# Delta rule on one Trainium2 core: the triangular inverse kept on one side and transposed for the other, with half the columns in each level

## The reference, cut to what matters

```python
a_mat = jnp.where(strict, jnp.einsum('bnhcd,bnhsd->bnhcs', k_beta, k) * gamma, 0.0) \
    + jnp.eye(CHUNK, dtype=jnp.float32)
rhs = jnp.concatenate([v * beta[..., None], k_beta * jnp.exp(G)[..., None]], axis=-1)
sol = lax.linalg.triangular_solve(a_mat, rhs, left_side=True, lower=True, unit_diagonal=True)
...
def step(S, inp):
    qd, w_c, u_c, at, kt, dec = inp
    v_new = u_c - jnp.einsum('bhcd,bhde->bhce', w_c, S)
    o = jnp.einsum('bhcd,bhde->bhce', qd, S) + jnp.einsum('bhcs,bhse->bhce', at, v_new)
    S = S * dec[..., None, None] + jnp.einsum('bhcd,bhce->bhde', kt, v_new)
    return S, o
```

## Time and profile before

| | us |
|---|---|
| median of 3 runs | 1982.2 |
| lowest and highest of them | 1977.0, 1984.09 |
| the profiled execution, device time | 1981.22 |
| its span in the profile | 1979.9 |
| PE busy | 1785.5 (90%) |
| DVE busy | 1232.4 (62%) |
| ACT busy | 718.6 (36%) |
| POOL busy | 434.1 (22%) |

### The profile page before, as it was taken

One profiled execution on the slowest core, in us unless ns is written; L12 is line 12 of the kernel. 1 busy time (PEld: TensorE's weight loads), 2 busy tenths in 40 slices (PEclk: granted clock), 3 DMA queues, 4 the chain that ended last, 5 costly groups with the idle time before them and its releaser, 6 DMA issues. The chain is left out here.

```text
span 1979.9 us, 23713 instructions
## 1 busy us (share of the span) xinstructions
PE 1785.5 (90%) x9424; PEld 1353.9 (68%) x9424; DVE 1232.4 (62%) x2155; ACT 718.6 (36%) x1243; POOL 434.1 (22%) x373
## 2 busy tenths in 40 slices
PE   7989999999999999998989999997878787887878
PEld 6869988977799879888979777893333333333333
DVE  4766655665576557654464445688776677667754
ACT  3545534344355346642342344343221122212211
POOL 0330000310000000004022000033555545454541
PEclk9989999999999999989989979998889988888889
DMA  6334555444445543412221211479999999999995
GB/s 261 110 114 149 191 183 180 170 153 166 165 176 190 182 177 110 149 64 80 92 68 62 86 62 67 170 287 421 422 421 421 422 422 421 422 422 421 421 422 245
DMA packets 62621, 453.76 MB, mean 229 GB/s; under 512 B 6944, under 2 KB 7072, under 8 KB 7856
## 3 DMA queue, kind: packets, MB, share of 16 engines
q0 software_dynamic: 36864, 268.45, 32.6%
q1 hardware_dynamic: 25040, 178.27, 25.4%
q10 hardware_dynamic: 608, 5.53, 0.7%
HBM read 451.18 MB, written 1.05 MB: 228 GB/s over the span
## 5 line engine op out<-in xcount | busy, mean ns | idle before, releaser
L2346 PE MATMUL banks<-uv_rows,diag 128*128 128x512 f32 x1024 | 509.8, 662 | 126.9 <-ACT diag L2395 122.5
L553 DVE TENSOR_TENSOR weights_lo<-weights,weights_hi 128x1024 fp32r<-128x1024 f32 x336 | 422.7, 1299 | 284.9 <-ACT weights_hi L544 282.3
L2346 PEld LDWEIGHTS banks<-uv_rows,diag 128*128 128x128 f32 x1024 | 215.4, 214 | 420.6 <-issue 269.3
L544 ACT ACTIVATE weights_hi<-weights 128x1024 fp32r<-128x1024 f32 x336 | 336.7, 1051 | 388.5 <-PE banks L560 380.2
L558 PE MATMUL banks<-x_hi,weights_hi 128*128 128x256 f32 (+1 forms) x1472 | 428.6, 291 | 6.7 <-DVE weights_lo L553 3.6
L560 PE MATMUL banks<-x_hi,weights_lo 128*128 128x256 f32 (+1 forms) x1472 | 422.0, 287 | 0.0
L559 PE MATMUL banks<-x_lo,weights_hi 128*128 128x256 f32 (+1 forms) x1472 | 421.8, 287 | 0.0
L2482 DVE CUSTOM_DVE_ANT_0 uv_rows<-uv_rows,tokens 128x1024 f32<-128x1024 f32 x256 | 306.4, 1224 | 165.1 <-DMA uv_rows<-expert_uv,index 165.0
L2505 POOL DMA_INDIRECT uv_rows<-expert_uv,index x256 | 310.9, 1214 | 339.9 <-PE banks L2346 285.5
L558 PEld LDWEIGHTS banks<-x_hi,weights_hi 128*128 128x128 f32 x1472 | 283.9, 193 | 16.8 <-issue 8.2
L560 PEld LDWEIGHTS banks<-x_hi,weights_lo 128*128 128x128 f32 x1472 | 283.6, 193 | 0.0
(11 more groups left out here) (379 smaller groups left out, 2239.8 us busy)
## 6 DMA issues: line engine op xcount, KB each, us to landing
weights<-weights SPq DMA_DIRECT2D x168, 1024.0 KB, 4.8
uv_rows<-expert_uv,index POOLq DMA_INDIRECT x256, 18.5
sb_first<-constants_first ACTq DMA_DIRECT2D x1, 1920.0 KB, 8.6
sb_always<-constants_always ACTq DMA_DIRECT2D x1, 1659.0 KB, 15.1
sb_peer<-constants_peer ACTq DMA_DIRECT2D x1, 1544.0 KB, 6.5
h<-x SPq DMA_DIRECT2D x1, 1024.0 KB, 5.7
out<-h SPq DMA_DIRECT2D x4, 256.0 KB, 4.7
sb_now<-constants_now ACTq DMA_DIRECT2D x1, 216.0 KB, 4.7
```

The costliest lines, as they stand in the source:

```text
L544: self.act.activation(self.w_hi[b % SLOTS][:, f], self.raw[b % SLOTS][:, f], ACT.Copy).then_inc(self.hi_made, 1)
L553: self.dve.tensor_tensor(self.w_lo[b % SLOTS][:, f], self.raw[b % SLOTS][:, f], self.w_hi[b % SLOTS][:, f], ALU.subtract).then_inc(self.lo ...
L2346: mm = pe.matmul(self.bank(2 * t + half), self.diag[:, k, :], self.uv[n % NUV][:, f], start=(u < NT and k == 0), stop=(u >= UNITS - NT and ...
```

## The change

- Only dTT is kept. dT is made anew in each level: PE transposes dTT into the tile's second bank, ACT copies it out as dT next to dM. The second product of step 4 (line 1797) and DVE's subtraction from dT (line 1965) are gone.
- In each level only the columns of the second blocks of each pair change in dTT. `second` names these columns (half of them), and M, dM, the remaining product and the subtraction are made for them alone: 64 columns instead of 128 for each head.
- In level 6 of tiles 1 and 2 (`whole`) the matrices are taken as squares of 64 by 64: A's lower left block is read where it stands, without the mask, and dB is not made.
- dTT starts as identity minus (dAT times "next"), two DVE operations for each tile inside the loop over tiles. The copies of the identity, the first dT, the first dB by the mask of level 0, POOL's part of it and the wait of all engines for T0 and T0_pool are gone. PE waits for the three dA instead, then for the tile's T0. POOL makes dB of level 1 for each tile as soon as that tile's dA is there and the last products with dgam are done.

The diff, cut to its core:

```diff
+    def second(self, x, lvl):
+        return x.rearrange("p h (b two s) -> p h b two s", two=2, s=1 << lvl)[:, :, :, 1, :]
+    def joined(self, lvl, t, j):
+        n = TILES[t][1]
+        return self.level_bank(t, j)[:, 0:HG * n // 2].rearrange("p (h b s) -> p h b s", h=HG, s=1 << lvl)
+    def whole(self, lvl, t):
+        return t > 0 and lvl == self.LEVELS[t] - 1
...
 tensor_delta:
-        wait("T0", 2)
-        wait("T0_pool", 1)
+        wait("A", 3)
         for lvl in range(1, 7):
             for t in self.active(lvl):
...
-                wait("B", i)
                 if lvl > 1:
                     wait("T", self.level_count(lvl - 1, t))
+                else:
+                    wait("T0", t + 1)
                 for hh in range(HG):
-                    mm = pe.matmul(ps[:, hh * n:(hh + 1) * n], b[:, hh, :], tt[:, hh, :], start=True, stop=True)
+                    if self.whole(lvl, t):
+                        pe.transpose(turned[0:half, hh * half:(hh + 1) * half], tt[0:half, hh, 0:half], C["ident"][0:half, 0:half])
+                    else:
+                        pe.transpose(turned[:, hh * n:(hh + 1) * n], tt[:, hh, :], C["ident"][0:n, 0:n])
+                if not self.whole(lvl, t):
+                    wait("B", i)
+                for hh in range(HG):
+                    if self.whole(lvl, t):
+                        mm = pe.matmul(ps[0:half, hh, 0, :], a[half:P, hh, 0:half], tt[half:P, hh, half:P], start=True, stop=True)
+                    else:
+                        mm = pe.matmul(ps[:, hh], b[:, hh, :], self.second(tt, lvl)[:, hh], start=True, stop=True)
...
                 for hh in range(HG):
-                    if not last:
-                        pe.matmul(pz[:, hh * n:(hh + 1) * n], m1[:, hh, :], tm[:, hh, :], start=True, stop=True)
-                    mm = pe.matmul(pzt[:, hh * n:(hh + 1) * n], tm[:, hh, :], m1[:, hh, :], start=True, stop=True)
+                    if self.whole(lvl, t):
+                        mm = pe.matmul(pzt[0:half, hh, 0, :], tm[0:half, hh, 0:half], m1[0:half, hh, 0:half], start=True, stop=True)
+                    else:
+                        mm = pe.matmul(pzt[:, hh], tm[:, hh, :], m1[:, hh, 0:n // 2].rearrange("p (b s) -> p b s", s=1 << lvl),
+                                       start=True, stop=True)
...
 scalar_delta:
-                act.activation(self.of("dM", t), self.level_bank(t, 0)[:, 0:HG * n].rearrange("p (h n) -> p h n", h=HG),
+                act.activation(self.of("dM", t)[0:rows, :, 0:n // 2],
+                               self.level_bank(t, 0)[0:rows, 0:HG * n // 2].rearrange("p (h n) -> p h n", h=HG), ACT.Copy)
+                act.activation(self.of("dT", t)[0:rows, :, 0:cols],
+                               self.level_bank(t, 1)[0:rows, 0:HG * cols].rearrange("p (h n) -> p h n", h=HG),
                                ACT.Copy).then_inc(d["M1"].sem, 1)
...
 vector_delta:
-            step.of(dve.tensor_copy(self.of("dT", t), self.each("ident", n)))
-            dve.tensor_copy(self.of("dTT", t), self.each("ident", n)).then_inc(d["eye"].sem, 1)
...
+            wait("masked", t + 1)
+            step.of(dve.tensor_tensor(self.of("dTT", t), at, self.each("next", n), ALU.mult))
             dve.wait_ge(step.sem, step.n)
-            step.of(dve.tensor_tensor(self.of("dT", t), self.of("dT", t), self.of("dB", t), ALU.subtract))
-            step.of(dve.tensor_tensor(self.of("dM", t), self.of("dAT", t), self.each("next", n), ALU.mult))
-            dve.wait_ge(step.sem, step.n)
-            dve.tensor_tensor(self.of("dTT", t), self.of("dTT", t), self.of("dM", t), ALU.subtract).then_inc(d["T0"].sem, 1)
+            dve.tensor_tensor(self.of("dTT", t), self.each("ident", n), self.of("dTT", t), ALU.subtract).then_inc(d["T0"].sem, 1)
...
-                if not final:
-                    step.of(dve.tensor_tensor(tm, tm, pz[:, 0:HG * n].rearrange("p (h n) -> p h n", h=HG), ALU.subtract))
-                    dve.wait_ge(step.sem, step.n)
-                dve.tensor_tensor(tt, tt, pzt[:, 0:HG * n].rearrange("p (h n) -> p h n", h=HG), ALU.subtract).then_inc(d["T"].sem, 1)
+                wait(*(("T", self.level_count(lvl - 1, t)) if lvl > 1 else ("T0", t + 1)))
+                dve.tensor_tensor(tt, tt, pzt, ALU.subtract).then_inc(d["T"].sem, 1)
...
 gpsimd_delta:
+        wait("prod_used", 3)
         for lvl in range(1, 7):
             for t in self.active(lvl):
+                if self.whole(lvl, t):
+                    continue
                 n = TILES[t][1]
                 if lvl > 1:
                     wait("M", self.level_count(lvl - 1, t))
+                else:
+                    wait("A", t + 1)
                 pool.tensor_tensor(self.of("dB", t), self.of("dA", t), self.each("merge", n, lvl * P), ALU.mult).then_inc(d["B"].sem, 1)
```

More of the change, by code:

```diff
@@ L492, in signals @@
         names = {"rows": 3, "rows_used": 3, "gam": 3, "prod": 3, "prod_used": 3, "turn": 3, "turn_used": 3, "masked": 3, "attn": 2,
-                 "back": 3, "A": 3, "eye": 3, "T0": 2, "T0_pool": 1, "B": 15, "M": 15, "M1": 15, "Z": 15, "T": 15, "ks": 2,
+                 "back": 3, "A": 3, "T0": 3, "B": 13, "M": 15, "M1": 15, "Z": 15, "T": 15, "ks": 2,
                  "rhs": 2, "pv": 3, "vn": 3, "sp": 2, "po": 2, "state": 2, "out": 2}
@@ L1865, in scalar_delta @@
         fill(7)
[L1866 to L1867 removed]
         for lvl in range(1, 7):
             for t in self.active(lvl):
[L1870 removed]
+                n, i, whole = TILES[t][1], self.level_count(lvl, t), self.whole(lvl, t)
+                rows, cols = (P // 2, P // 2) if whole else (n, n)
                 act.wait_ge(d["M"].sem, d["M"].at(group, i))
[L1872 removed]
+                act.activation(self.of("dM", t)[0:rows, :, 0:n // 2],
+                               self.level_bank(t, 0)[0:rows, 0:HG * n // 2].rearrange("p (h n) -> p h n", h=HG), ACT.Copy)
+                act.activation(self.of("dT", t)[0:rows, :, 0:cols],
+                               self.level_bank(t, 1)[0:rows, 0:HG * cols].rearrange("p (h n) -> p h n", h=HG),
                                ACT.Copy).then_inc(d["M1"].sem, 1)
@@ L1957, in vector_delta @@
             for t in self.active(lvl):
-                n, i, final = TILES[t][1], self.level_count(lvl, t), lvl == self.LEVELS[t] - 1
-                tm, tt = self.of("dT", t), self.of("dTT", t)
-                pz, pzt = self.level_bank(t, 1), self.level_bank(t, 2)
+                i = self.level_count(lvl, t)
+                tt, pzt = self.second(self.of("dTT", t), lvl), self.joined(lvl, t, 2)
+                if self.whole(lvl, t):
+                    tt, pzt = (x[0:P // 2] for x in (tt, pzt))
                 wait("Z", i)
-                if lvl > 1:
-                    wait("T", self.level_count(lvl - 1, t))
-                if not final:
-                    step.of(dve.tensor_tensor(tm, tm, pz[:, 0:HG * n].rearrange("p (h n) -> p h n", h=HG), ALU.subtract))
-                    dve.wait_ge(step.sem, step.n)
-                dve.tensor_tensor(tt, tt, pzt[:, 0:HG * n].rearrange("p (h n) -> p h n", h=HG), ALU.subtract).then_inc(d["T"].sem, 1)
+                wait(*(("T", self.level_count(lvl - 1, t)) if lvl > 1 else ("T0", t + 1)))
+                dve.tensor_tensor(tt, tt, pzt, ALU.subtract).then_inc(d["T"].sem, 1)
             fill(7 + 2 * lvl)
@@ L2004, in wait @@
             pool.wait_ge(d[name].sem, d[name].at(group, n))
-        n = TILES[2][1]
-        wait("A", 3)
-        wait("eye", 3)
-        wait("masked", 3)
-        step.of(pool.tensor_tensor(self.of("dB", 2), self.of("dA", 2), self.each("merge", n), ALU.mult))
-        pool.wait_ge(step.sem, step.n)
-        step.of(pool.tensor_tensor(self.of("dT", 2), self.of("dT", 2), self.of("dB", 2), ALU.subtract))
-        step.of(pool.tensor_tensor(self.of("dM", 2), self.of("dAT", 2), self.each("next", n), ALU.mult))
-        pool.wait_ge(step.sem, step.n)
-        pool.tensor_tensor(self.of("dTT", 2), self.of("dTT", 2), self.of("dM", 2), ALU.subtract).then_inc(d["T0_pool"].sem, 1)
-        wait("T0", 2)
-        wait("T0_pool", 1)
+        wait("prod_used", 3)
         for lvl in range(1, 7):
             for t in self.active(lvl):
+                if self.whole(lvl, t):
+                    continue
                 n = TILES[t][1]
```

22 lines of the change are left out of this document (5 added, 17 removed).

## The result

| | before | after |
|---|---|---|
| median of 4 runs, us | 1981.54 | 1954.84 |
| lowest and highest | 1977.0, 1984.09 | 1952.89, 1965.39 |
| the profiled execution, device time | 1981.22 | 1965.39 |
| its span | 1979.9 | 1964.1 |

After over before is 0.9875, with a 95% interval of 0.9839 to 0.9911. The kernel is faster by 26.7 us between medians, where 38.6 were forecast. 1954.84 lies inside the range, 12 us above the forecast and near the times of rivals 1 and 2. The profiled execution is the slowest of the four, so its total is compared with nothing here; its stretches are. One execution of a later kernel (3522.3 us, at half clock throughout) was in a disturbed state and is left out everywhere.

A forecast was written before the change was run, and what follows sets the result against it. PE's own program order bounds the levels, except waits for POOL before level 1. 25.0 + 2.6 + 9.5 + 4.0 - 2.5 = 38.6 us less gives 1943 us; own range 1938 to 1949, wide range 1936 to 1961.

The forecast's parts named there:

- rival 1: Handovers, POOL's masks and splits collide; each of the 12 levels loses 1 us more than forecast: 1955 us, chance 0.16.
- rival 2: Half the columns don't take half the time; stationary load or strided read sets 0.112 us a record: 1959, chance 0.15.
- Part 1: Levels 1 to 5, tiles 1 and 2: half columns, 0.124 us a product, no second product; 25.0 us less.
- Part 2: Level 6 in 64 by 64 squares: 1.15 us against 1.79, four times; 2.6 us less (1.4 to 2.7).
- Part 4: Start of level 1: PE's waits for POOL's dB go, all three inputs being early; 9.5 us less.
- Part 5: Without the 4 us pause before level 1, the half clock behind it should not come: 4.0 us less, at least 0.
- rival 4: Slower: thin work drops the clock to 1.2 GHz, 2018 us, chance 0.03; partial form, group 1 levels, 1949, 0.07.
- Part 6: Handovers to ACT and DVE in the levels make PE wait, against 3.8 us of old idle time: net cost 2.5 us.
- Part 7: Weight stream: with two slots, the chain of ACT and DVE making a block's parts fits in the levels; nothing counted.
- The last sign: The prediction is wrong if the time between the delta rule and the end changes, which the change doesn't touch.

## Why the prediction was right, and where its sum was not

The sign, the range and the mechanisms of the start held; the size did not. The forecast's own range, 1938 to 1949, missed the time. The wide range held it because it took in rivals 1 and 2; that the time lies at rival 1's 1955 is chance, since that rival's mechanism didn't appear. The gain is accounted for at equal clock, from the traces of before and after. In the levels the length less half of the half-clock time went from 62.9 to 56.6 us in group 0 (64.6 less 1.7; 60.0 less 3.4) and from 48.3 (51.1 less 2.8) to 40.5 in group 1: 14.1 us. The stretches from the first key product to level 1, read the same way, went down by 8.2 us. These are their rows before and after:

```profile
855.22:898.91 43.69, 37.47 (x269) 33.84 (x269) 26.65 (x49) 20.98 (x47) 8.49 (x6) 0.96 0.25 93
990.30:1034.09 43.79, 37.76 (x270) 34.00 (x270) 29.08 (x50) 21.90 (x47) 7.41 (x6) 0.91 0.21 73
```

```profile
852.90:892.45 39.55, 37.40 (x269) 33.81 (x269) 22.29 (x39) 18.67 (x44) 4.28 (x3) 0.96 0.27 99
980.40:1022.93 42.53, 40.41 (x270) 36.84 (x268) 26.06 (x42) 21.43 (x46) 3.65 (x3) 0.84 0.19 67
```

The stretches of group 0 differ by 4.1 us at one clock, 0.96. In group 1 the length times the clock is 39.8 and 35.7, 4.1 less. DVE's and POOL's busy time fell as their copies and masks went. Together with the levels that is 22.3 us.

**Part 1 is the step that failed: "I take 0.062, so 0.124 a product".** The record of 128 stationary and 64 moving columns steps at 0.112 us, the upper bound. The part gives 9.0 us, not 25.0; what PE saves is the second product of step 4, less the transposes, and no columns. The choice between the bounds went by the row with the same load, but that row's operation was a transpose, and the sizes of a row don't carry over to another kind of operation. This is rival 2 in its full form, and the Trainium skill, page "TensorE: Matmul & The Clock Gate", section "LDWEIGHTS (loading the stationary operand)", had it: by its rule a load of 128 columns takes 107 ns whatever the partitions, and the products here, at 0.112 on 128 partitions and on 8, agree. The transposes with the same 128 columns, at 0.063, do not. I had set that one row against the rule where the rule applied.

**Part 2.** The square level takes 0.94 us for transposes and M and about 0.52 for the product (8 records at 0.065), 1.46 a tile where I took 1.15. Against the 1.79 of before, four times, it saves 1.3 us of PE's time, not 2.6. The run without squares doesn't measure this sum, since it puts half columns at full height there and not the two full products of before: its tile takes about 2.2 us, 2.9 more in the four places, where the traces have 2.7 and the means 4.

**Part 4.** All three conditions were early, as forecast. The waits of 8.0 and 1.5 us are gone, and the stretches ahead of level 1 are 8.2 us shorter at equal clock. By the runs with one part alone the start is worth more than this part and part 5 together, 18 us against 13.5.

**Part 5.** Half right. The half clock behind the pause is gone, and in the kernel with the new start and the old levels a run has 20 us less of it, worth 7 to 10 us. In the changed kernel it came back: behind level 6 of both groups, and ahead of level 1 of group 1, where the rows above go from 0.91 to 0.84. The mean half-clock time of a run is 251 to 259 us, against 254: the net is nothing, not 4.0. This is the partial form of rival 4, at other places. In group 0 the clock fell behind the wait of 1.0 us in all three traces of the changed kernel and in none with that wait filled, but two other kernels with the same wait kept it. So what makes it fall stayed open, in group 0 in part and in group 1 wholly: there it also falls with full columns and with level 6 at full height.

**Part 6.** The handovers cost less. The table of waits of the changed kernel, PE between 860 and 1100 us, has this row for the products of level 6:

```profile
PE banks L1819 <- ACT dT L1897: 1.3, 2, 1.0
```

That, 1.3 us in two waits, and 0.5 us before the recurrence is all, 1.8 us. Level 6 of group 0 waits 1.0 us instead of about 1.8. The 0.27 and 0.45 us that I expected between M and the product in levels 2, 3 and 5 are not there. M of tile 2, which PE makes meanwhile, takes 0.84 us instead of the 0.50 that Part 1 gave it, and the product of tile 1 is longer in the same way; that this is what covers them was argued, not tried. Against 3.8 us of old idle time the part gives 2.0 us more instead of costing 2.5. Rival 1 is out: no wait for POOL's dB stands in the levels. (Its argument that DVE's load falls by two thirds was too high: in the levels it fell from 53.4 to 29.7 us.)

**The sum with these terms**, parts 1, 2, 4, 6 and 5 in this order, is 9.0 + 1.3 + 9.5 + 2.0 + 0 = 21.8 us, against 22.3 in the two traces' delta rule and 22 to 25 by the three ratios. Two errors of the forecast had opposite signs, the pace (16 too much) and the handovers (4.5 too little). That the two partly cancel is luck and not foresight: with the pace right and all else as forecast it would have been rival 2's 1959. Part 7 held: the projections' weights didn't hold PE in the levels. The last sign, the time behind the levels, is 894.7 us before and 900.6, 894.0 and 898.7 in the three traces of the changed kernel. It lies around the old value, and the spread is as large within one kernel.

## What to carry to other kernels

With 128 stationary columns, a step of f32 products was shortened only when the stationary side shrank with the moving one; take a triangular or block structure as squares, not as column halves. When a product's pace is read from a neighbouring row, check the kind of operation as well as the sizes: a transpose is no product. And a removed pause can be worth more than its idle time if the clock fell behind it, but that part is kept only if the clock doesn't fall elsewhere in the new schedule: compare the half-clock time of whole runs, not the one stretch.

## What the runs showed of the hardware

- An f32 product with 128 stationary columns takes 0.112 us a record with 64 or 16 moving columns on 128 partitions and with 8 on 8 partitions; with 64 and 64 columns 0.058 to 0.065; with 32 and 32 columns 0.031.
- A transpose of f32 data with 128 stationary columns and 8 or 64 moving ones takes 0.062 to 0.063 us, and its weight-load record 0.137 us against 0.187 for a product of the same sizes.
- A wait of 1.0 us between small squares was followed by 6.8 us at 1.2 GHz in all three traces of the changed kernel, but the same wait was followed by 2.4 GHz in the kernels with full columns and with the old start. With eight unread records in that wait the stretch ran at 2.4 GHz in both traces. The time at half clock over a whole run was 237 and 248 us with them, against 251 to 259; the three runs of the first are few.
- Within one kernel a run's time rises by about 0.34 us for each us more at half clock, over the 120 runs whose clock is on record.
